# Two transformer blocks on one core: the scan's first columns on GpSimd, gating and the bonus product later, queries in quarters, choices placed anew

## The reference

```python
mod = (c_act @ ada_w[l] + ada_b[l])[:, None, :]
h = rms_norm(x, norm_mix_g[l]) * (1.0 + sc1) + sh1
p = h @ w_in[l]
y_a = rwkv7_mixer(...)           # 4 heads of 64, state recurrence, a bonus sum(r*k*r_k) * v
y_b = spatial_gating_mixer(...)  # layer norm, then a masked 128x128 product per group
y_c = short_conv_mixer(...)
y_d = s5_mixer(...)              # complex diagonal recurrence over the 256 tokens (an associative scan)
gates = jax.nn.sigmoid(p[..., OFF_G:]).reshape(bsz, seq, N_BRANCH, D_MODEL)
merged = gates[:, :, 0] * y_a + gates[:, :, 1] * y_b + gates[:, :, 2] * y_c + gates[:, :, 3] * y_d
x = x + gt1 * (merged @ w_o[l])
...
x = x + gt2 * (jnp.square(jax.nn.relu(h @ ffn_w1[l])) @ ffn_w2[l])
```

```python
qh = (xt @ w_peer_q).reshape(T, PEER_HEADS, 2, PEER_HALF)
s = jnp.einsum('thpd,hpnd->thpn', qh, sub_keys)
sv, si = lax.top_k(s, 16)            # per head and half, of 128 keys
best, pick = lax.top_k(cand, 16)     # of the 256 sums of the two halves
u = expert_u[ic]
hval = jnp.einsum('cd,chkd->chk', xc, u)
a = gc * jax.nn.gelu(hval, approximate=False)
out = jnp.einsum('chk,chkd->cd', a, expert_v[ic])
```

## Time and profile before

| | |
|---|---|
| Median of 3 runs | 1496.22 us (1494.41 to 1498.22) |
| Profiled execution | 1487.54 us, span 1486.2 us |
| Mean granted clock of TensorE | 0.926 |
| PE busy | 1233.5 us, 83% |
| DVE busy | 936.0 us, 63% |
| ACT busy | 396.5 us, 27% |
| POOL busy | 366.6 us, 25% |
| DMA | 484.32 MB, 326 GB/s over the span |

### The profile page before, as it was taken

The page is one execution under the profiler, slowest core; times in us unless marked ns, Lnnn a source line. Parts: engine busy times, 40 slices in busy tenths (PEclk is TensorE's granted clock), DMA queues, the critical chain, the costliest instruction groups (busy, mean ns, idle before and its releaser), DMA issues.

```text
span 1486.2 us, 14391 instructions
## 1 busy us (share of the span) xinstructions
PE 1233.5 (83%) x4994; PEld 761.1 (51%) x4994; DVE 936.0 (63%) x2028; ACT 396.5 (27%) x1048; POOL 366.6 (25%) x285
## 2 busy tenths in 40 slices
PE   4988999999999999988777486967489878777776
PEld 2875656564767775487644265433284333333322
DVE  5188877973210221166667899897678777776654
ACT  2152111121101222112112222443224433333323
POOL 0001121201000000023334232433247444443430
PEclk9999999999999999998888688689699998999999
DMA  9633344465796665479999999899999999999996
GB/s 372 266 139 127 114 149 177 170 227 226 286 357 277 241 238 215 177 303 426 421 425 426 420 423 412 370 413 425 375 395 415 421 421 421 422 420 421 421 421 260
DMA packets 56089, 484.32 MB, mean 326 GB/s; under 512 B 6480, under 2 KB 8784, under 8 KB 10192
## 3 DMA queue, kind: packets, MB, share of 16 engines
q0 software_dynamic: 36864, 268.45, 43.7%
q1 hardware_dynamic: 18000, 211.35, 36.2%
q10 hardware_dynamic: 1152, 3.59, 0.6%
HBM read 482.32 MB, written 1.05 MB: 325 GB/s over the span
## 4 chain that ended last, share of the span: by engine, by line
PE 48%; DMA 28%; DVE 8%; issue 4%; ACT 2%; POOL 1%; SPq 0%; DVEq 0%; ACTq 0%
PE ps L490 27%; DMA arena<-in_euv,arena 12%; DMA ring<-in_euv,arena 7%; PE ps L869 6%; PE ps L578 6%; PE ps L947 5%; DMA ring<-in_w 5%; PE ps L1080 3%; DVE xr L1855 1%; DVE arena L1831 1%; DMA ring<-in_wout 1%; DMA ring<-in_qkv 1%; DMA ring<-in_pq 1%; DMA ring<-in_bb 1%; DVE arena L1406 1%
## 5 line engine op out<-in xcount | busy, mean ns | idle before, releaser
L2424 POOL DMA_INDIRECT arena<-in_euv,arena x161 | 202.0, 1255 | 621.1 <-DVE arena L1786 307.6
L490 PE MATMUL ps<-arena,ring 128*128 128x128 f32 (+1 forms) x1680 | 249.8, 314 | 50.5 <-DMA ring<-in_w 22.5
L490 PEld LDWEIGHTS ps<-arena,ring 128*128 128x128 f32 x1680 | 236.1, 211 | 68.5 <-DMA ring<-in_w 26.0
L1831 DVE CUSTOM_DVE_ANT_0 arena<-arena 128x1024 f32<-128x1024 f32 x161 | 195.1, 1223 | 58.3 <-DMA arena<-in_euv,arena 56.4
L490 PE MATMUL ps<-arena 128*128 128x128 f32 (+5 forms) x1340 | 196.3, 301 | 27.4 <-issue 12.9
L1080 PE MATMUL ps<-arena 128*128 128x512 f32 x356 | 177.2, 646 | 48.0 <-ACT arena L2296 47.1
L490 PEld LDWEIGHTS ps<-arena 128*128 128x128 f32 (+1 forms) x1340 | 171.4, 195 | 62.4 <-issue 54.2
L1080 PEld LDWEIGHTS ps<-arena 128*128 128x128 f32 x356 | 70.8, 205 | 152.4 <-issue 81.6
L2320 ACT ACTIVATE arena<-arena 128x2 f32<-128x2 f32 x127 | 25.7, 203 | 426.1 <-DVE arena L1831 420.7
L1831 DVE CUSTOM_DVE_ANT_0 ring<-ring,arena 128x1024 f32<-128x1024 f32 x75 | 91.3, 1221 | 45.8 <-DMA ring<-in_euv,arena 45.7
L1080 PE MATMUL ps<-ring,arena 128*128 128x512 f32 x216 | 101.5, 610 | 21.6 <-ACT arena L2296 21.3
(11 more groups left out here) (331 smaller groups left out, 1278.7 us busy)
## 6 DMA issues: line engine op xcount, KB each, us to landing
ring<-in_w SPq DMA_DIRECT2D x24, 2048.0 KB, 7.5
ring<-in_ada SPq DMA_DIRECT2D x10, 2048.0 KB, 7.5
ring<-in_qkv SPq DMA_DIRECT2D x9, 2048.0 KB
ring<-in_gates SPq DMA_DIRECT2D x8, 2048.0 KB, 7.7
arena<-in_w SPq DMA_DIRECT2D x6, 2048.0 KB, 11.0
ring<-in_g SPq DMA_DIRECT2D x6, 2048.0 KB
ring<-in_pq SPq DMA_DIRECT2D x6, 2048.0 KB
ring<-in_wp SPq DMA_DIRECT2D x5, 2048.0 KB, 8.2
```

The costliest lines, as they stand in the source:

```text
L490: ins = te.matmul(o, l, r, start=(i == 0), stop=(i == len(pairs) - 1))
L1831: ins = v.tensor_tensor_reduce(out=x, in0=x, in1=xn[:, tt, :], scale=1.0, scalar=0.0, op0=ALU.mult, op1=ALU.add, accum_out=hv[:, n % 16:n ...
L2424: gp.indirect_dma_start(slots[i], None, A["euv"], bass.IndirectOffsetOnAxis(ap=idx[:, n // 16 % 4, e % 16:e % 16 + 1].bitcast(U32), axis=0 ...
```

## The change

It has six parts.

1. The eight copies of first columns of pass n = 0 go from ScalarE to GpSimd (a new generator `s5` there). Those of passes 1 to 3 stay.
2. Gating has one more `yield` on TensorE, VectorE and ScalarE: the root of the layer norm and the two sums `sg` come one step later.
3. `bon` is made behind the four products of tt = 0, in rwkv's step 5, instead of in step 4. `SCHEDULE` puts rwkv's steps 5 to 13 one place later; from step 14 on the places are the same.
4. The first head's queries and scores are made in quarters of 128 columns: `qp0.0a`, `qp0.0`, `sc0.0a`, `sc0.0`, and the first choice starts on the scores of the first quarter.
5. `strewn` and `chosen_at` place the picks of steps 2 to 15 by a table of costs on VectorE. Picks 5.0 to 7.3 were at groups 24, 26, ... 46; now they are at 25, 30, 31, 32 (step 5), 33, 36, 39, 40 (step 6) and 41, 42, 45, 48 (step 7).
6. The keys' load for tt = 1 moves from ahead of `wout` part 1 to ahead of `pq` part 0.

```diff
 SCHEDULE = [...
-            "ad", "ad", "ad", "ad", "ad", "a", "add", "a", "ad", "ad", "d", "ad", ...
+            "ad", "d", "ad", "ad", "ad", "a", "add", "a", "ad", "ad", "ad", "ad", ...

+def chosen_at(before):
+    work = [sum(ON_VECTOR.get(u[:2], ON_VECTOR.get(u[:1], 0)) for u in units) for units in before] + [0] * 16
+    scored = next(g for g in range(GROUPS) if ("pq", 0) in before[g]) + 1
+    at, free = {}, 0
+    for s in range(2, len(STEPS)):
+        lo = max((s - 2) * PER_STEP, free, scored if s >= 8 else 0)
+        lo = min(lo, (s - 1) * PER_STEP - 2) if s < 8 else lo
+        near = range(lo, max((s - 1) * PER_STEP + 1, lo + 4))
+        best = min(itertools.combinations(near, 4), key=lambda gs: (
+            sum(work[g] + (work[g - 1] if g else 0) for g in gs) + sum(6 for a, b in zip(gs, gs[1:]) if b == a + 1), gs))
+        for q, g in enumerate(best):
+            at.setdefault(g, []).append((s, q))
+        free = best[-1] + 1
+    return at

 # TensorE
             def gating():
                 yield
                 yield
+                yield
                 te.wait_ge(sig("vln"), 1)
...
-                o = take("bon", "misc")
-                te.wait_ge(sig("rk"), 1)
-                for tt in range(2):
-                    for c in range(2):
-                        ins = mm(o[:, 4 * tt + 2 * c:4 * tt + 2 * c + 2], [(tmp[:, c, tt * 128:(tt + 1) * 128], hsel)])
-                ins.then_inc(*fill("bon"))
                 yield
...
                     heads(f"Mrk{tt}", kt_, rm, tt)
+                    if tt == 0:
+                        o = take("bon", "misc")
+                        te.wait_ge(sig("rk"), 1)
+                        for h in range(4):
+                            ins = mm(o[:, 2 * h:2 * h + 2], [(tmp[:, h % 2, h // 2 * 128:(h // 2 + 1) * 128], hsel)])
+                        ins.then_inc(*fill("bon"))
                     yield
...
-                o = take("qp0.0", "main")
-                for c in range(2):
-                    ins = queries(o, c, c)
-                ins.then_inc(*fill("qp0.0"))
+                queries(take("qp0.0a", "main"), 0, 0).then_inc(*fill("qp0.0a"))
+                queries(take("qp0.0", "main"), 1, 0).then_inc(*fill("qp0.0"))
+                scored("sc0.0a", 0, 1)
                 o = take("qp0.0b", "main")
                 queries(o, 2, 0)
-                te.wait_ge(*empty("qp0.0"))
-                scored("sc0.0", 0)
+                scored("sc0.0", 1, 1)

 # VectorE, choose(n)
-                v.wait_ge(*empty("sc0.0b" if n == 1 else f"sc{tt}.{h // 2}"))
+                v.wait_ge(*empty(f"sc{tt}.{h // 2}" if n > 1 else ("sc0.0a", "sc0.0b")[n]))
...
                 for s in range(2):
+                    if n + s == 1:
+                        v.wait_ge(*empty("sc0.0b" if n else "sc0.0"))

 # ScalarE, s5
-                        tell(sc.copy(dst[:, :, :, 0:s_], src[:, :, :, 0:s_]), "s5_head")
+                        if n:
+                            tell(sc.copy(dst[:, :, :, 0:s_], src[:, :, :, 0:s_]), "s5_head")

 # GpSimd
+            def s5():
+                for _ in range(5):
+                    yield
+                src, dst = xa, xb
+                for lv in range(8):
+                    s_ = 1 << lv
+                    if lv == 0:
+                        gp.wait_ge(*empty("bu0.1"))
+                    else:
+                        gp.wait_ge(sig("s5_level"), lv)
+                        gp.wait_ge(sig("s5_head"), lv)
+                    gp.tensor_copy(dst[:, :, :, 0:s_], src[:, :, :, 0:s_]).then_inc(sig("s5_head"), 1)
+                    src, dst = dst, src
+                    yield

 # SP
-                    if key == (("pq", 0, 0), ("wout", 1, 1))[tt]:
+                    if key == ("pq", 0, tt):
                         sy.wait_ge(*full(f"bo1.{tt}1"))
                         sy.wait_ge(sig("merged2"), 2 * tt + 2)
                         sy.dma_start(keys, A["keys"][0]).then_inc(sig("l_keys"), 16)
```

78 lines of the change are left out of this document (41 added, 37 removed).

## The result

The changed kernel takes 1486.83 us (median of 4 runs, 1485.59 to 1490.28); the kernel before takes 1497.22 us beside it (4 runs, 1494.41 to 1498.96). The ratio is 0.9935, with a 95% interval of 0.9915 to 0.9955: faster by 9.7 us (6.7 to 12.7), which is clear of the 0.3%.

The account below looks back on a forecast made before the run. Engines bound the kernel up to the first gather, transfers after it. Terms 1.0 + 5.2 - 2.05 - 6.0 = -1.85 us take the profiled 1487.54 to 1485.7; with the median 8.7 above, 1494.4 us, range 1487 to 1503.

Parts of the forecast that it names:

- Two kernels in a row: Engines decide up to the first gather at 651.48, transfers from there to 1470.70; VectorE busy 46.13 of 47.30 us in 92.77 to 140.07.
- By elements +1.0 us: Scan's first columns: GpSimd's copies disturb VectorE's levels in proportion to 508 elements, costing 1.0 us.
- +5.2 us: First stretch: masks behind ada(4) delay the fourth product, D0 and the next sy; 5.2 us later, between 0 and 7.2.
- -2.05 us: Queries in quarters: first MAX8 starts on the first quarter's scores, so gathers come 2.05 us sooner, between 0 and -2.7.
- Together -6.0 us: Second stretch: strewn picks and the moved keys' load fill transfer holes at 960 and 1060 to 1080; between +4.7 and -7.6.
- the hole of 960: Transfers idle 4.6 us in 960 to 970, with VectorE busy 9.52 of 10 us; moved picks to recover 3 us.
- It would take 1485.7: Whole kernel: the profiled execution of 1487.54 us less 1.85; the median, 8.7 above, is forecast at 1494.4.
- A: Second stretch: strewn picks in groups 30 to 33 make a hole of their own; +8.85, 1505.1 us; chance 0.15.
- B: First stretch: the masks' delay is hidden, next sy near 195; -7.05, 1489.2 us; chance 0.20.
- C: Scan: GpSimd disturbs VectorE by the instruction, 6.4 for 1.0 us; +3.55, 1499.8 us; chance 0.10.
- D: Second stretch: nothing changes and the holes stay; +4.15, 1500.4 us; chance 0.13.
- the holes' upper bound, -7.6 us: Second stretch: the most that filling holes could gain, 7.6 us idle by DMA share in the windows near 960 and 1060 to 1080.

Follow-up runs that it names:

- `copies_gating`: Kernel before with the scan's first-column copies on GpSimd and gating's root and sums one step later; ratio 1.0008 to the kernel before.
- `copies`: Kernel before with only the scan's first-column copies moved from ScalarE to GpSimd; ratio 1.0019 to the kernel before.
- `sched_back`: Whole change except the new SCHEDULE, which is that of the kernel before; ratio 0.9927 to the kernel before.
- `mixer`: Kernel before with GpSimd copies, gating later, bonus later and rwkv's steps 5 to 13 one place later; ratio 1.0018 to the kernel before.
- `again`: The kernel before once more, with no edit; 1495.35 us, ratio 0.9998.
- `picks`: Kernel before with only the picks placed by chosen_at; ratio 0.9971 to the kernel before.
- `keys`: Kernel before with only the keys' load moved behind the second wout load; ratio 0.9976 to the kernel before.

## Why the prediction was right or wrong

**Two kernels in a row, VectorE the bound in 92.77 to 140.07:** right. `copies_gating` takes TensorE's wait away and gains nothing.

**"By elements +1.0 us":** nearly right in size and wrong in place. The levels don't grow (1.66 and 1.60 us), but the two TENSOR_SCALARs beside the copies of 256 and 512 elements do, by 0.65 to 0.67 us, in all six profiles with the copies and in none of the others. VectorE reaches the end of level 128 0.70 us later with the copies alone and 0.85 with all parts. GpSimd itself gave way once (0.70 us in `copies` for the copy that takes 0.30 in the change). The rows from which I had the price were of instructions of 512 elements with two operands; where such stand beside a level in the changed kernel, at 153.74, the four L1427 take 3.58 us against 2.51 before and 1.67 undisturbed. The Trainium skill ("GPSIMD Engine Reference", section 1) names two kinds of VectorE instruction that contend with GpSimd, those with two SBUF inputs and those in a 2-port perf mode. L1427 bears out the first beside GpSimd's products; whether the two TENSOR_SCALARs are of the second kind no row here shows.

**"+5.2 us" for the masks behind `ada(4)`:** the mechanism was right, each instruction in its place, and the size nearly: the second `sy` came at 200.92 (6.1 later) where 199.6 to 200.5 was said, since D0 came at 157.04 and not 155.5. That is the masks, at 150.98 in place of 149.1: level 128 ends 1.1 us later than I had put it (the 0.85 above, and 0.26 by which this execution is late already at the first level), and VectorE waits 1.37 us for ScalarE ahead of the mix where I had 0.6. The first `sy`, slowed to 3.35 us behind a wait of 11.42, isn't in it. With the +1.0 of the copies the sum said 6.2 us for the second `sy`, and 6.1 came. Over the whole stretch it is 4.4 to 5.7 us against the two profiles of before and 5.9 as an average of all profiles, of which the schedule holds about half (`sched_back`), and by time 2.7 (-0.6 to +5.8).

**"-2.05 us" for the quarters:** right: 2.1 us in the trace (from L2192, 637.32, to MAX8, 642.90, 5.58 us; from L2220, 641.60, to 645.06, 3.46), 1.9 at the first gather, 2.7 (0.4 to 4.8) by time.

**"Together -6.0 us" for picks and keys:** this is the term that failed, in two ways. The 3 us of the hole of 960 didn't come. I had read it as VectorE's backlog, from 9.52 busy us in the window of 960; the wait of 2.80 us for TensorE's scores ends at 959.78, just ahead of that window. The hole did not shrink (6.2 us against 4.6); what the traces show ahead of it is VectorE's wait for TensorE's scores at the lower clock (2.80 us before, 3.18 in the change), and where that wait is absent, in `mixer`, the hole is 2.5 us. And behind 1060 the hole was sized too small. The shares said 3.0 us; by bytes it was 6.8 in the same profile and 8.4 as an average of the six with the old order, and the picks and the keys' load took nearly all of it. The keys' part was right in place: -3.0 in the sum, 3.6 (2.1 to 5.1) measured. The picks, for which I had nothing there, gave 4.3 us (2.5 to 6.0). The second stretches of six profiles with the old order take 838.1 us on average, those of four profiles with picks and keys 830.2: -7.9, and -4.3 - 3.6 = -7.9 by time.

**"It would take 1485.7", and the median 8.7 above it:** the time of the profiled execution came out at that (1485.59 for 1485.7), which is luck, since the terms of the two stretches were off by 1.8 and 1.7 us in opposite directions. The step that failed with it is to carry a difference from that execution to the median. The profiled execution of before lies 8.7 us under its median, that of the change 1.2. Its second stretch was the shortest of six, 3.4 us under their average, so what the change could win there was read too small; and its first gather came 3.5 to 4.9 us sooner than in the three other profiles of kernels with the same first stretch (`again`, `picks`, `keys`). With the measured parts, -2.7 - 4.3 - 3.6 + 2.7 = -7.9 us, within the interval of the result (-12.7 to -6.7).

**The rivals.** A didn't come: the picks in groups 30 to 33 make no hole. B, the masks' delay hidden, is refuted by the second `sy` at 200.92; that its time (1489.2) was nearest is luck. C and D are refuted by the rows. That the range just failed to hold the time lies in the holes' upper bound, -7.6 us, taken from one profile and from shares alone; the next profile had 12.8 us by the same count.

## What to carry to other kernels

One profiled execution is one draw. Where it lies 9 us under the median of the runs, the time that is missing from it is in the medians, and a change that removes waits can win a part of it back (3.4 us of it were in the second stretch here); ask for the holes of a usual run before the bound of such a term is set, and size them by the bytes moved as well as by the share. A window's busy time doesn't show a wait that ends just ahead of it.

Freeing an engine that is ahead of the bound moves its wait and doesn't shorten it (3.64 us became 9.40), and the work behind the longer wait can run at the lower clock. A load that waits for a late event should stand behind the loads that don't (the keys' load: 3.6 us).
